# A hybrid decoder step on one core: residual x kept in DRAM during the cache loop, its room used as a second ring for key pages

## The reference

```
h   = rms_norm(x, norm1[l]);  proj = h @ w_in[l]          # q, k, v, z, xbc, dt, xp
past_k = cache_k[l][page_table];  past_v = cache_v[l][page_table]
z = einsum(q, k) * scale + bias                           # stick-breaking attention over past and new keys
log_keep = where(mask, log_sigmoid(-z), 0)
w = where(mask, exp(log_sigmoid(z) + later(log_keep)), 0)
o = einsum(w, v)
...                                                       # y_ssd (state space) and y_pool (pooling)
x = x + concat([o, y_ssd, y_pool]) @ w_out[l]
x = x + (silu(conv(h2 @ w_gate[l])) * (h2 @ w_up[l])) @ w_down[l]    # h2 = rms_norm(x, norm2[l])
```

## Time and profile before

| | us |
|---|---|
| three runs: median (lowest to highest) | 3244.02 (3238.09 to 3248.26) |
| the profiled execution | 3247.16 |
| span of its trace, first to last instruction | 3245.5 |
| PE busy | 3158.5, 97% of the span |
| cache loop, layer 0 / layer 1 (from the trace) | about 312 to 586 / 1910 to 2191 |
| TensorE clock granted, mean | 0.991 of full speed |

### The profile page before, as it was taken

The page is one execution under the profiler, slowest core; times in us unless marked ns, Lnnn a source line. Parts: engine busy times, 40 slices in busy tenths (PEclk is TensorE's granted clock), DMA queues, the critical chain, the costliest instruction groups (busy, mean ns, idle before and its releaser), DMA issues.

```text
span 3245.5 us, 62265 instructions
## 1 busy us (share of the span) xinstructions
PE 3158.5 (97%) x23688; PEld 3020.3 (93%) x23688; DVE 1898.0 (58%) x3325; ACT 1346.5 (41%) x1663; POOL 428.2 (13%) x541
## 2 busy tenths in 40 slices
PE   8999998999999999999999999989999999999998
PEld 7999676999999999999999986769999999999998
DVE  5574756466654665466656657555666446644654
ACT  4463666334433333333335546563443333333332
POOL 0000754110000000000300026532100000000002
PEclk9999999999999999999999999999999999999999
DMA  6443799644454445444544448986444444444443
GB/s 201 134 130 108 259 330 332 192 143 155 142 157 143 155 144 156 150 152 135 160 138 130 130 128 276 337 280 189 148 147 155 146 154 146 151 148 152 143 147 107
DMA packets 470007, 554.34 MB, mean 171 GB/s; under 512 B 21279, under 2 KB 415232, under 8 KB 469700
## 3 DMA queue, kind: packets, MB, share of 16 engines
q1 hardware_dynamic: 442339, 467.07, 45.0%
q0 software_dynamic: 27104, 84.75, 7.7%
q10 hardware_dynamic: 385, 0.14, 0.0%
HBM read 535.50 MB, written 16.38 MB: 170 GB/s over the span
## 4 chain that ended last, share of the span: by engine, by line
PE 90%; DVE 2%; DMA 2%; ACT 2%; issue 1%; PEld 1%; DVEq 1%; POOL 0%; SPq 0%; POOLq 0%; ACTq 0%; PEldq 0%
PE ps L1165 26%; PE ps L1167 26%; PE ps L1166 26%; PE ps L1409 3%; PE ps L1421 1%; PE ps L1453 1%; DMA kring<-in_cache_k 1%; PE ps L1561 1%; PE ps L1571 1%; DMA vring<-in_cache_v 1%; PE ps L1498 1%; PE ps L1435 0%; ACT L963 0%; DMA raw<-in_w_out 0%; ACT kT L949 0%
## 5 line engine op out<-in xcount | busy, mean ns | idle before, releaser
L1679 DVE TENSOR_TENSOR wl<-raw,wh 128x1024 fp32r<-128x1024 f32 (+1 forms) x736 | 901.0, 1234 | 989.0 <-ACT wh L782 982.4
L782 ACT ACTIVATE wh<-raw 128x1024 fp32r<-128x1024 f32 (+1 forms) x736 | 764.5, 1041 | 1587.2 <-PE ps L1167 1573.8
L1165 PE MATMUL ps<-fh,wh 128*128 128x320 f32 x2816 | 870.6, 309 | 0.0
L1167 PE MATMUL ps<-fh,wl 128*128 128x320 f32 x2816 | 870.1, 309 | 0.0
L1166 PE MATMUL ps<-fl,wh 128*128 128x320 f32 x2816 | 870.1, 309 | 0.0
L1166 PEld LDWEIGHTS ps<-fl,wh 128*128 128x128 f32 x2816 | 528.6, 188 | 0.2
L1165 PEld LDWEIGHTS ps<-fh,wh 128*128 128x128 f32 x2816 | 528.6, 188 | 0.2
L1167 PEld LDWEIGHTS ps<-fh,wl 128*128 128x128 f32 x2816 | 528.6, 188 | 0.0
L1165 PE MATMUL ps<-ah,wh 128*128 128x320 f32 x1376 | 427.0, 310 | 0.0
L1167 PE MATMUL ps<-ah,wl 128*128 128x320 f32 x1376 | 425.2, 309 | 0.0
L1166 PE MATMUL ps<-al,wh 128*128 128x320 f32 x1328 | 410.3, 309 | 0.0
(11 more groups left out here) (408 smaller groups left out, 3742.0 us busy)
## 6 DMA issues: line engine op xcount, KB each, us to landing
raw<-in_w_gate SPq DMA_DIRECT2D x88, 1024.0 KB, 5.1
raw<-in_w_up SPq DMA_DIRECT2D x88, 1024.0 KB, 5.0
raw<-in_w_in SPq DMA_DIRECT2D x72, 1024.0 KB, 5.2
kring<-in_cache_k SPq DMA_DIRECT2D x256, 256.0 KB, 4.7
vring<-in_cache_v POOLq DMA_DIRECT2D x256, 256.0 KB, 5.0
raw<-in_w_down SPq DMA_DIRECT2D x64, 1024.0 KB, 5.3
raw<-in_w_out SPq DMA_DIRECT2D x32, 1024.0 KB, 7.2
raw<-in_w_down SPq DMA_DIRECT2D x32, 768.0 KB, 4.6
```

Source lines behind the costliest of these rows:

```text
L782: act.activation(wh[:, s % 2, half, :], raw[:, s, half, :], ACT.Copy).then_inc(hi_done, 1)
L1165: pe.matmul(out, wh[:, s % 2, kk, w], hi(row), start=first, stop=False)
L1167: mm = pe.matmul(out, wl[:, s % 2, kk, w], hi(row), start=False, stop=last)
L1679: dve.tensor_tensor(wl[:, s % 2, half, :], raw[:, s, half, :], wh[:, s % 2, half, :].bitcast(F32), ALU.subtract).then_inc(lo_done, 1)
```

## The change

The last 16 KB of the 20 KB of `x` in each partition (`x_late`, 2 MB in all) are written to a DRAM tensor `x_kept` once the planes of the layer are made; POOL issues this ahead of its first meeting. Their room becomes `kring[0]`, the old ring is `kring[1]`. Even chunks use the one, odd chunks the other. SP waits for the store, loads the first chunk's 8 pages ahead of the units of `B_XP`, the second chunk's pages where the first's were before, and then page k of chunk q when page k of chunk q-2 has been transposed. The state loads stay at the same `k_T` count. After `first_out(1)` SP issues the load of `x_late` back from `x_kept`; DVE waits for it (`x_back`) after the meeting and ahead of `out_lo(3)`. One semaphore now stands for a pair of key pages.

```diff
+        x_at = at[0]
         x = sb("x", [P, KT, TOK])
...
-        kring = sb_at("kring", [P, RING, SBW], F32, raw_at)
+        kring = [sb_at("kring0", [P, RING, SBW], F32, x_at + 4096), sb_at("kring1", [P, RING, SBW], F32, raw_at)]
+        x_late = x[:].rearrange("p k t -> p (k t)")[:, 1024:1024 + RING * SBW]
+        x_kept = nc.dram_tensor("x_kept", (P, RING * SBW), F32, kind="Internal").ap()
...
-        k_loaded = [sem(f"k_loaded{i}") for i in range(RING)]
+        k_loaded = [[sem(f"k_loaded{i}_{j}") for j in range(RING // 2)] for i in range(2)]
+        x_stored, x_back = sem("x_stored"), sem("x_back")
...
+                def key_in(q, k):
+
+                    at_page = (q // 4 * 2 + k // 4) * PAGES + 4 * (3 - q % 4) + k % 4
+                    page = sync.value_load(pages[0:1, at_page:at_page + 1], min_val=0, max_val=a["cache_k"].shape[1] - 1)
+                    sync.dma_start(kring[q % 2][:, k, :], a["cache_k"][l, page].rearrange("s h d -> s (h d)")
+                                   ).then_inc(k_loaded[q % 2][k // 2], 16)
+
+                sync.wait_ge(x_stored, 16 * (l + 1))
+                for k in range(RING):
+                    key_in(0, k)
                 body(l, B_XP, a["w_in"], 0, 8, XPC, XPC + 256)
...
-                for q in range(CHUNKS):
+                for q in range(1, CHUNKS):
                     for k in range(RING):
-                        slot = RING * (q - 1) + k
-                        if q == 0:
+                        slot = RING * (q - 2) + k
+                        if q == 1:
                             sync.wait_ge(lo_done, (l * BODIES + B_XP + 1) * 8 + 2 * (k // 4) + 2)
                         else:
                             sync.wait_ge(k_T, l * (CHUNKS * 8) + (slot + 1))
...
+                        key_in(q, k)
...
                 first_out(1)
+                sync.dma_start(x_late, x_kept).then_inc(x_back, 16)
                 sync.wait_ge(q_mm, l * GROUPS + GROUPS)
...
+                pool.wait_ge(h_hi, l * 32 + KT)
+                pool.wait_ge(h_lo, l * 32 + KT)
+                pool.dma_start(x_kept, x_late).then_inc(x_stored, 16)
                 meet(pool, "pool", stage(l, M_IN))
...
-                    pe.wait_ge(k_loaded[k], l * (16 * CHUNKS) + 16 * (q + 1))
+                    pe.wait_ge(k_loaded[q % 2][k // 2], l * (16 * CHUNKS) + 32 * (q // 2 + 1))
...
                 meet(dve, "dve", stage(l, M_MIX))
+                dve.wait_ge(x_back, 16 * (l + 1))
```

More of the change, by code:

```diff
@@ L1408, in key_page @@
                     for j in range(SBT):
-                        mm = pe.transpose(ps[4 + n % 2][:, j * P:(j + 1) * P], kring[:, k, j * P:(j + 1) * P], ident)
+                        mm = pe.transpose(ps[4 + n % 2][:, j * P:(j + 1) * P], kring[q % 2][:, k, j * P:(j + 1) * P], ident)
                     mm.then_inc(k_T, 1)
```

## The result

| | before | changed |
|---|---|---|
| median of 20 runs, us | 3242.7 | 3249.2 |
| lowest to highest | 3232.8 to 3248.3 | 3242.7 to 3260.1 |
| profiled execution / its span, us | 3247.2 / 3245.5 | 3260.1 / 3258.5 |
| mean granted clock of the profiled execution | 0.991 | 0.986 |

The ratio is 1.0024 (95% interval 1.0016 to 1.0032): slower by 7.8 us, 5.2 to 10.4 (the two medians alone differ by 6.5 us). By the bound of 0.3% that is still no change; by the interval it is a loss.

The account below looks back on a forecast made before the run. PE was taken to bound the kernel, busy 97% of the span, with gaps in the cache loop. Keys -5.3 and tail +7.4 gave +2.1 us: 3246.1 on the median 3244.0, stated as 3247; range 3240 to 3253, with rivals 3236 to 3256.

Parts of the forecast that it names:

- within 0.3%: Whole kernel: time the same as before within the bound of 0.3%, 9.7 us; chance 0.80.
- The tail: End of both cache loops: `x_late` gets ahead of value pages PE waits for; 4.5 + 4.5 - 1.6 = 7.4 us.
- The 1.6 us that I gave back in layer 1: Layer 1's loop end: waits for chunk 15's pages get covered as PE comes later; 1.6 us of 2.4 returned.
- I take 4.5 us per layer: Loop end: delay of value pages 6 and 7 of chunk 14 by `x_late`, between nothing and 7.5 us, 9.4 at most.
- turns: Loop end, rival: value pages take their turn beside `x_late`; tail 0 to 1 us per layer, about 3240; chance 0.22.
- The 0.94 us that I took from q8's packets: Loop end: time per 16 KB row, range 0.70 to 1.17; eight rows per DMA engine 7.5 us.
- The keys: Middle of the cache loops: the second ring removes PE's key waits; 5.3 us gained, bounds 2.8 to 8.7.
- The sign that I had named, 15 to 15.6 us: Layer 0's cache loop: chunk 9 would last this long, not 18.1 us, if the forecast was right.
- the chunk's length also holds what PE lost while pages came one by one: Cache loops: reason for taking 5.3 us from chunk lengths against 15.0 us, above the 2.8 us of idle time.
- What was priced at nothing: Store, eight early page loads, waits for key-page pairs and DVE's wait for `x_back`: all hidden, 0 us.
- Slow block: Loop end, rival: `x_late` goes ahead whole at q8's dearest rows; 9.4 us per layer, +11.9, 3256; chance 0.11.
- The keys' time isn't won: Cache loop, rival: states or value pages next in line keep chunk 9 long; 0 + 7.4, about 3251; chance 0.10.

Follow-up runs that it names:

- `tail_alone`: Kernel before, one key ring and its key loads kept, plus the store of `x_late` and its reload behind the second `B_OUT` unit: 3252.3 us, ratio 1.0025.
- `chunk0_behind`: Changed kernel with the first chunk's eight key loads behind the units of `B_XP` instead of ahead of them: 3253.1 us, ratio 1.0034.
- `rows2k`: Changed kernel with `x_kept` stored and reloaded in rows of 2 KB instead of 16 KB, same bytes and place: 3242.9 us, ratio 0.9998.
- `early16k`: Changed kernel with the 16 KB-row reload some 13 us earlier, ahead of the first two units of `B_OUT`: 3240.5 us, ratio 0.9994.
- `after_again`: Changed kernel run once more, unaltered, for a second profile, against the kernel before: 3248.6 us, ratio 1.0028.
- `swap`: Changed kernel with 2 KB rows, rings changed over, two `B_OUT` units a chunk earlier, reload behind the third: 3241.3 us, ratio 1.0001; second run 3239.6, 0.9992.

## Why the prediction was right, and where its sizes were off

**The time.** 3247 us was forecast and 3249.2 measured, inside the range, and "within 0.3%" was the likeliest case. But I forecast +2.1 us from the change, and it is +7.8 (5.2 to 10.4). That 3247 lies so near is in part luck: the base of three runs, 3244.0, was 1.3 us above the median of the 20, and 0.9 us had been added for leaning to the dearer rows. Two terms were mis-sized, both to the same side.

**The tail, +7.4 forecast, 9 to 12 us shown.** Place, pages and cause are as forecast: pages 6 and 7 of chunk 14, behind `x_late`, in both layers. PE's wait for value pages grew by 5.5 us in layer 0 (8.0 - 2.5) and 4.7 in layer 1 (7.1 - 2.4) of the first profile, against 4.5 and 2.9. The 1.6 us that I gave back in layer 1 did come: the waits for chunk 15's pages are gone, both that are left are chunk 14's. But these two pages alone went there from 0.8 us (2.4 - 1.6) to 7.1, 6.3 more where I had 4.5. In the second profile the waits grew by only 4.0 and 2.2 us, and PE was busy for 18.3 and 17.5 us with the 209 matmuls that took it 15.4 and 16.1 before, at lower clocks: a term that the sum did not have. Over both layers the waits grew by 10.2 and 6.2 us in these two profiles and by 10.8 and 10.1 in `tail_alone` and `chunk0_behind`; 7.4 was too little for three of the four. The step that failed here is "I take 4.5 us per layer", between a free tail and all of `x_late` ahead: the second page did wait for practically all of it.

How `x_late` came ahead was between my two pictures, a block or turns. The turns are there, row by row, with rows of 16 KB (65 of 66 followed by a packet of the other queue) and, for the most part, of 2 KB (116 of 141, `rows2k`, 567 to 571 us). I read "turns" as a free tail: the 0 to 1 us per layer in that rival was my estimate and no row or run shows it; PE's waits grew by 5.5 and 4.7 us. With one long row (0.62 us) against one short packet (0.18 us) turns are nearly a block: shared evenly, the 128 rows of `x_late` are eight of 16 KB for each of the 16 DMA engines, and the two pages of 256 KB are eight rows of 4 KB for each, so `x_late` would be through about when the second page is; that page landed 0.3 us before it. Eight rows at 0.62 us are 5.0 us, an estimate that needs only the sizes of the rows of two queues and the time of one. The 0.94 us that I took from q8's packets was no measure of these rows.

**The keys, -5.3 forecast.** The waits for key pages went in both loops, and the ten key loads in a row stay, as said. The length of the chunks was the wrong measure. The windows of chunk 9 of layer 0, from key page to key page, first of before:

```profile
453.46:471.58 18.12, 16.73 (x171) 13.02 (x170) 8.03 (x13) 9.66 (x15) 7.59 (x11) 0.91 1.00 359
```

of the changed kernel, layer 0:

```profile
459.45:475.85 16.40, 16.30 (x170) 12.96 (x169) 8.12 (x13) 9.54 (x15) 7.56 (x10) 0.91 1.05 371
```

and of `rows2k`, with the same two rings:

```profile
456.31:471.37 15.06, 14.96 (x171) 11.79 (x170) 8.13 (x13) 9.44 (x15) 7.58 (x10) 1.00 1.05 375
```

At a clock of 1.00 the chunk without late keys lasts 15.06 us, as forecast; at 0.91 it lasts 16.40. Before the change it ran at 0.91 too. So of the 3.1 us that I read as keys, 16.40 - 15.06 = 1.3 were the clock, and 18.12 - 16.40 = 1.7 the keys; whether the key wait itself brought the lower clock with it is not shown. The sign that I had named, 15 to 15.6 us, came in `rows2k` and not in the changed kernel (16.40 and 15.99 us). The step that failed here is "the chunk's length also holds what PE lost while pages came one by one": it also holds the clock, which the same view prints and which I did not set beside the length. Layer 1's 1.2 and 1.0 us stood at 1.00 and hold in `rows2k` (15.06 us for both chunks, at 1.00); in the changed kernel chunk 12 lasted 15.06 us there too, but chunk 9 16.67 and 16.20, at clocks of 0.90 and 0.93. Then chunk 8 got longer, 13.63 to 14.30 us in layer 0 and 14.09 to 14.54 in layer 1 (`rows2k`, all four at a clock of 1.00), as PE's wait for ACT's weights at its end grew from 0.27 to 0.94 us and from 0.74 to 1.19. Net: 1.7 + 1.2 + 1.0 - 0.7 - 0.4 = 2.8 us, which is the lower bound that I had set. As the executions ran, each with its own clock, chunks 8, 9 and 12 of both layers took 93.2 us before and 91.8 and 92.3 in the two profiles of the changed kernel, 1.4 and 0.9 less; `tail_alone`, with one ring, took 92.5. There is one profile of the kernel before, so the size stays open between about 1 and 2.8 us. With 9.2 to 11.7 us for the tail that makes +6.4 to +10.8, around the +7.8 measured.

**What was priced at nothing.** The store took 8.2 and 8.8 us to land and nothing waited for it; the first key page of layer 0 comes at 313.7 us, before the change at 313.9; from 215 to 312 us ACT's waits name PE, 17 times, 43.5 us, as in the earlier trace rows. DVE's wait ahead of `out_lo(3)` still ends with ACT (7.7 us), not with `x_kept`, though `x_late` took 14 us. `chunk0_behind` and the chunks' lengths show no price of the eight early loads.

**The rivals.** *Turns* had the mechanism right and the price wrong, since I did not weigh the length of the rows. *Slow block* had the place and, for the second page, nearly the whole transfer ahead of it, but its rows took 0.62 us and not q8's, so its price of 9.4 us per layer was too much. Its sign, `x_late` taking over 9 us, did come (13.7 and 14.3), and it told nothing: the unit in front and the turns make up the length, as 8.9 and 8.3 us in `early16k` show. *The keys' time isn't won* is half true: ACT's weights, not states or value pages, are next in line and take about 1.1 us of the 3.9 back (`rows2k` against before).

## What to carry to other kernels

Before a transfer is put beside others that an engine waits for, compare the rows of both. Here the queues took turns packet by packet, so a transfer with rows of 16 KB, 0.62 us each, took more than four bytes of five (1.04 MB of 1.23) from one with rows of 4 KB, 0.18 us each; cutting its rows to 2 KB cost nothing that the times show (0.9998) and turned that round (0.69 MB beside 0.89). When a late stretch is priced by its length, set the granted clock beside the length, in that stretch and in the one it is compared with: here the same chunk took 15.06 us at 1.00 and 16.40 at 0.91. And look first for what made the data late: here one number in the order of the loads left no wait for a key page in its profile either, without 2 MB of buffer and two transfers, though neither way gained time that can be told from none.

## What the runs showed that I had not expected

- Rows of 16 KB were not slower to move by themselves (0.62 us, against 0.18 us for one of 4 KB, four of which are as many bytes): alone at the head of its queue the reload of 2.1 MB took 8.3 and 8.9 us (`early16k`), behind a unit 13.1 to 14.8, and in rows of 2 KB behind a unit and beside value pages 18.6 and 20.1, at no cost to the kernel that its times show.
- In the four profiles with a wait of 3.9 to 6.0 us at the end of layer 0's loop (changed, `after_again`, `tail_alone`, `chunk0_behind`) the granted clock was at 0.50 for some 10 us, from within PE's waits for value pages on, in the profile of before for some 3.4. The end of the loop can then be longer by more than the waits: in `after_again` it was 6.3 us longer with waits 4.0 us longer, and PE needed 18.3 us for 209 matmuls that took 15.4 before, at a mean clock of 0.74 against 0.92. In the first profile of the changed kernel half of that stretch fell into the waits themselves, and they took 16.1 us; in `rows2k`, with no wait above 2.0 us there, they took 17.0 at 0.84. So a lower clock stood there without the long wait, too.
- The mean clock over the runs (without one at 0.747 of `swap` and one at 0.761 of the kernel before) is lower for the versions with the long wait: 0.9903, 0.9907, 0.9897 and 0.9888 (changed, `after_again`, `tail_alone`, `chunk0_behind`), against 0.9915 to 0.9929 for the others, 0.9910 to 0.9919 for the kernel before in the three sessions. Across the runs of one kernel 0.001 less of mean clock went with 1.7 to 2.6 us more (the slope of a line through the runs of each version). That the wait causes this is not shown beyond the windows above.
